# Prompt row tiles found in two waves, with a third strand for the first wave's attention heads

## The reference, cut to what matters

```
def blk(args):                       # 128 query rows at a time, 8 such row tiles
    qb, iqb, iwb, qpos = args
    sc = index_scores(iqb, iwb, ik, key_pos[None, :] <= qpos[:, None])
    vals, idx = lax.top_k(sc, n_sel)             # n_sel = 256
    k_sel, v_sel = k[idx], v[idx]                # abridged
    return sparse_attend(qb, k_sel, v_sel, jnp.isfinite(vals))   # 8 heads

def rwkv7_scan(...):                 # 1024 steps, 4 heads, state S[v, k]
    sa = einsum('bhvk,bhk->bhv', S, at)
    S = S * dt + sa * bt + vt * kt
```

## Time and profile before

| what | value |
|---|---|
| median of 3 runs | 7837.82 us (7829.0 to 7849.85) |
| the profiled execution | 7838.83 us |
| its span, first to last instruction | 7837.1 us |
| busy in the span: TensorE, VectorE, ScalarE | 6192.6, 3201.9, 1222.3 us |
| `stage_prompt_mix`, layer 0 and layer 1 | 963 us each |
| mean granted TensorE clock of the span | 0.799 |

### The profile page before, as it was taken

One profiled execution on the slowest core, in us unless ns is written; L12 is line 12 of the kernel. 1 busy time (PEld: TensorE's weight loads), 2 busy tenths in 40 slices (PEclk: granted clock), 3 DMA queues, 4 the chain that ended last, 5 costly groups with the idle time before them and its releaser, 6 DMA issues. The chain is left out here.

```text
span 7837.1 us, 64844 instructions
## 1 busy us (share of the span) xinstructions
PE 6192.6 (79%) x23434; PEld 3851.3 (49%) x23434; DVE 3201.9 (41%) x7042; ACT 1222.3 (16%) x2304; POOL 737.2 (9%) x776
## 2 busy tenths in 40 slices
PE   7979436558987599999989785365499876999997
PEld 4534324446686445554455334234467863455543
DVE  2246335895452023330032553458944510333300
ACT  2200212112301011110032003121133011111100
POOL 3300000000034400000032000000000353000000
PEclk9989556556667799999999895565567588999999
DMA  4222111000022421112132220110000223211122
GB/s 139 73 75 74 35 31 39 29 13 12 10 59 65 140 106 52 50 53 64 56 112 79 79 70 20 28 48 19 13 18 5 58 76 134 106 56 50 46 73 93
DMA packets 358057, 462.88 MB, mean 59 GB/s; under 512 B 70258, under 2 KB 261172, under 8 KB 357332
## 3 DMA queue, kind: packets, MB, share of 16 engines
q1 hardware_dynamic: 320932, 358.82, 14.2%
q0 software_dynamic: 36864, 100.71, 4.2%
HBM read 347.87 MB, written 121.69 MB: 60 GB/s over the span
## 5 line engine op out<-in xcount | busy, mean ns | idle before, releaser
L395 PE MATMUL pp<-w_in,nT 128*128 128x512 f32 x2016 | 947.0, 618 | 0.0
L2808 PE MATMUL pg<-nT,wgu 128*128 128x512 f32 (+1 forms) x2112 | 709.2, 489 | 17.1 <-DMA wgu<-in_w_up 17.1
L2808 PE MATMUL pu<-nT,wgu 128*128 128x512 f32 (+1 forms) x2112 | 704.4, 487 | 0.0
L2879 PE MATMUL pm<-w_down,hT 128*128 128x512 f32 x1584 | 683.5, 595 | 24.6 <-DMA hT<-scratch_hT 24.6
L2402 POOL DMA_INDIRECT k_sel<-in_cache_k,kv_idx x256 | 243.9, 953 | 4049.8 <-DVE kv_idx L2535 3826.8
L395 PEld LDWEIGHTS pp<-w_in,nT 128*128 128x128 f32 x2016 | 390.8, 199 | 451.4 <-issue 450.7
L2808 PEld LDWEIGHTS pg<-nT,wgu 128*128 128x128 f32 x2112 | 351.6, 192 | 357.3 <-issue 357.3
L2808 PEld LDWEIGHTS pu<-nT,wgu 128*128 128x128 f32 x2112 | 349.8, 191 | 336.6 <-issue 336.6
L2879 PEld LDWEIGHTS pm<-w_down,hT 128*128 128x128 f32 x1584 | 302.2, 191 | 404.6 <-issue 404.6
L2188 DVE TENSOR_SCALAR_CACHE_REDUCE area<-score,cand 128x384 f32<-128x384 f32 x372 | 350.8, 943 | 9.1
L2831 DVE TENSOR_SCALAR sig<-exp_neg 128x512 f32<-128x512 f32 x132 | 47.6, 360 | 722.0 <-ACT exp_neg L2819 722.0
(11 more groups left out here) (581 smaller groups left out, 9128.4 us busy)
## 6 DMA issues: line engine op xcount, KB each, us to landing
w_in<-in_w_in SPq DMA_DIRECT2D x14, 2048.0 KB, 9.3
scratch_hT<-hT SPq DMA_DIRECT2D x44, 576.0 KB, 2.8
hT<-scratch_hT SPq DMA_DIRECT2D x18, 1408.0 KB, 7.4
wgu<-in_w_gate SPq DMA_DIRECT2D x44, 512.0 KB, 3.9
wgu<-in_w_up SPq DMA_DIRECT2D x44, 512.0 KB, 5.2
w_down<-in_w_down SPq DMA_DIRECT2D x22, 1024.0 KB
x_all<-scratch_x SPq DMA_DIRECT2D x27, 512.0 KB, 15.2
a_tile<-scratch_pa SPq DMA_DIRECT2D x18, 516.0 KB, 3.6
```

The costliest lines, as they stand in the source:

```text
L395: ins = pe.matmul(pp[u % 2][:, 0:cw], nT[:, k, t * P:(t + 1) * P], w[:, k, 0:cw], start=(k == 0), stop=(k == KT - 1))
L2808: ins = pe.matmul(bank[:, 0:cw], wb[b][:, which, k, :], nT[:, k, c0:c0 + cw], start=(k == 0), stop=(k == KT - 1))
L2879: ins = pe.matmul(pm[b][n][:, :], h[b][:, k, :], w[:, k, n * 512:(n + 1) * 512], start=(k == 0), stop=(k == FT - 1))
```

## The change

The searched row tiles are put into two waves, tiles 7 and 6, and tiles 5, 4, 3 and 2; the index part takes them in this order. The search is done for the first wave, 32 rounds and its picks, and then for the second. `dsa_strand` becomes `dsa_strands` and gives two strands, select (index, count, pick) and heads. Heads take the row tiles in the order 7, 6, 5, 4, 3, 2, 1, 0. Buffers of the two strands no longer share a tensor: `eq`, `rank`, `s`, `pr`, `pT` are tensors of their own, and the heads' VectorE part has a chain semaphore of its own. The order has three phases:

1. RWKV row tiles 0 and 1 beside the index part of all tiles and the first wave's search;
2. RWKV row tiles 2, 3, 4 beside the second wave's search and the first 32 steps of the heads (16 pairs, the heads of tiles 7 and 6);
3. RWKV row tiles 5, 6, 7 beside the other heads.

```
-def dsa_strand(nc, st, l, io, sc, const, bk):
+def dsa_strands(nc, st, l, io, sc, const, bk):
-    TOPPED = list(range(FIRST, NT))
+    WAVES = ((7, 6), (5, 4, 3, 2))
+    TOPPED = [i for wave in WAVES for i in wave]
+    ORDER = TOPPED + list(range(FIRST - 1, -1, -1))
+    place = {i: n for n, i in enumerate(ORDER)}
...
-    HEADS = [(i, h) for i in range(NT) for h in range(BH)]
+    HEADS = [(i, h) for i in ORDER for h in range(BH)]
...
-    area = st.sb("area", [P, 2, ALL])
-    eq, rank = area[:, 0, :], area[:, 1, :]
-    s = [area[:, 0, b * SEQ:(b + 1) * SEQ] for b in range(2)]
-    pr = [area[:, 0, (2 + b) * SEQ:(3 + b) * SEQ] for b in range(2)]
-    pT = [area[:, 1, b * SEQ:(b + 1) * SEQ] for b in range(2)]
+    eq, rank = st.sb("equal", [P, SEQ]), st.sb("rank", [P, SEQ])
+    s = [st.sb(f"s{b}", [P, SEQ]) for b in range(2)]
+    pr = [st.sb(f"p{b}", [P, SEQ]) for b in range(2)]
+    pT = [st.sb(f"pT{b}", [P, SEQ]) for b in range(2)]
...
-        def settle(r):
+        def settle(r, n0, n1):
+            m = slice(n0, n1)
...
-        for r in range(BITS + 1):
-            for n in range(NTOP):
-                if n == 0 and r:
-                    settle(r - 1)
-                    chain(dve.tensor_tensor(cand[:, :], thr[:, :], bit[:, r - 1:r].to_broadcast([P, NTOP]), ALU.bitwise_xor))
-                count(r, n)
-                yield
-        settle(BITS)
-        for n in range(NTOP):
-            for k in range(3):
-                pick(n, k)
-                yield
+        for wave in WAVES:
+            n0, n1 = TOPPED.index(wave[0]), TOPPED.index(wave[-1]) + 1
+            for r in range(BITS + 1):
+                for n in range(n0, n1):
+                    if n == n0 and r:
+                        settle(r - 1, n0, n1)
+                        chain(dve.tensor_tensor(cand[:, n0:n1], thr[:, n0:n1], bit[:, r - 1:r].to_broadcast([P, n1 - n0]), ALU.bitwise_xor))
+                    count(r, n)
+                    yield
+            settle(BITS, n0, n1)
+            for n in range(n0, n1):
+                for k in range(3):
+                    pick(n, k)
+                    yield
...
+    def heads_vector(dve):
+        chain = Chain(dve, heads_chain_s)
...
-        order = interleave(r_costs, d_costs)
+        tile = (len(r_costs) - 1) // NT
+        r_early, r_late = 2 * tile, 5 * tile
+        order = (interleave(r_costs[:r_early], s_costs[:s_mid], [])
+                 + interleave(r_costs[r_early:r_late], s_costs[s_mid:], h_costs[:h_mid])
+                 + interleave(r_costs[r_late:], [], h_costs[h_mid:]))
```

More of the change, by code:

```diff
@@ L1968, in rwkv_strand @@
     return tile * NT + [2.0], sync, scalar, tensor, vector
-def dsa_strand(nc, st, l, io, sc, const, bk):
+def dsa_strands(nc, st, l, io, sc, const, bk):
     FIRST = TOPK // P
-    TOPPED = list(range(FIRST, NT))
+    WAVES = ((7, 6), (5, 4, 3, 2))
+    TOPPED = [i for wave in WAVES for i in wave]
     NTOP = len(TOPPED)
+    ORDER = TOPPED + list(range(FIRST - 1, -1, -1))
+    place = {i: n for n, i in enumerate(ORDER)}
     BITS = 31
     width = lambda i: (i + 1) * P
-    off = {i: sum(width(j) for j in TOPPED if j < i) for i in TOPPED}
+    off = {i: sum(width(j) for j in TOPPED[:TOPPED.index(i)]) for i in TOPPED}
     ALL = sum(width(i) for i in TOPPED)
@@ L2017, in dsa_strand @@
     po, pt = bk[3], bk[2]
-    loaded, k_loaded, idx_p, idx_r, idx_used, s_p, s_r, mx_r, p_r, pt_p, pt_r, o_p, o_r, chain_s = (st.sem(n) for n in (
-        "ds_loaded", "k_loaded", "idx_psum", "idx_relu", "idx_added", "s_psum", "s_ready", "max_ready", "p_ready", "pT_psum", "pT_ready", "o_psum", "o_ready", "ds_dve_chain"))
+    loaded, k_loaded, idx_p, idx_r, idx_used, s_p, s_r, mx_r, p_r, pt_p, pt_r, o_p, o_r, chain_s, heads_chain_s = (st.sem(n) for n in (
+        "ds_loaded", "k_loaded", "idx_psum", "idx_relu", "idx_added", "s_psum", "s_ready", "max_ready", "p_ready", "pT_psum", "pT_ready", "o_psum", "o_ready", "ds_dve_chain", "heads_dve_chain"))
     stored = [st.sem(f"ds_stored{b}") for b in range(2)]
@@ L2034, in sync @@
         yield
-        for n in range(1, len(costs)):
+        for n in range(1, len(select_costs)):
             if n == 8:
@@ L2041, in sync, with heads_sync @@
                 sp.dma_start(v[:, :, :], sc["v"][0:SEQ, :].rearrange("(t p) n -> p t n", p=P)).then_inc(k_loaded, 16)
+            yield
+    def heads_sync(sp):
+        for n in range(len(heads_costs)):
             if n in out_at:
-                i = out_at[n]
-                sp.wait_ge(o_r, i + 1)
-                sp.dma_start(sc["y"][i * P:(i + 1) * P, AW:AW + BW], o[i % 2][:, :, :].rearrange("p h d -> p (h d)")).then_inc(stored[i % 2], 16)
+                p = out_at[n]
+                i = ORDER[p]
+                sp.wait_ge(o_r, p + 1)
+                sp.dma_start(sc["y"][i * P:(i + 1) * P, AW:AW + BW], o[p % 2][:, :, :].rearrange("p h d -> p (h d)")).then_inc(stored[p % 2], 16)
             yield
@@ L2058, in index, with heads_tensor @@
                 pe.matmul(bk[g % 4][:, 0:cw], iqT[e, h // 2, i * P:(i + 1) * P], ikT[e, c0:c0 + cw], start=True, stop=True).then_inc(idx_p, 1)
+        pe.wait_ge(loaded, 80)
+        for n in range(len(IDX)):
+            index(n)
+            yield
+        yield
+        yield
+        for n in range((BITS + 1) * NTOP + 3 * NTOP):
+            yield
+    def heads_tensor(pe):
         def score(H):
@@ L2083, in values @@
             pe.wait_ge(pt_r, part0[H + 1])
-            if h == 0 and i:
-                pe.wait_ge(o_r, i)
+            if h == 0 and place[i]:
+                pe.wait_ge(o_r, place[i])
             for k in range(i + 1):
@@ L2122, in relu, with heads_scalar @@
                 act.activation(rl[n % 2][:, c0:c0 + cw], bk[g % 4][:, 0:cw], ACT.Relu, scale=HD ** -0.5).then_inc(idx_r, 1)
+        yield
+        for n in range(len(IDX)):
+            relu(n)
+            yield
+        yield
+        for n in range((BITS + 1) * NTOP + 3 * NTOP):
+            yield
+    def heads_scalar(act):
         def expo(H):
@@ L2138, in turned @@
             act.activation(pT[H % 2][:, c0:c0 + cw], pt[:, 0:cw], ACT.Copy).then_inc(pt_r, 1)
[L2140 to L2146, removed]
         for H in range(len(HEADS) + LAG):
@@ L2175, in weigh @@
                 chain(dve.tensor_tensor(last, last, masks[:, CAUSAL_QK, :], ALU.add))
-        def settle(r):
+        def settle(r, n0, n1):
+            m = slice(n0, n1)
             if r == 0:
-                chain(dve.tensor_scalar(thr[:, :], cnt[:, :], TOPK - 0.5, -1.0, ALU.is_lt, ALU.mult))
+                chain(dve.tensor_scalar(thr[:, m], cnt[:, m], TOPK - 0.5, -1.0, ALU.is_lt, ALU.mult))
             else:
-                chain(dve.scalar_tensor_tensor(out=keep[:, :], in0=cnt[:, :], scalar=TOPK - 0.5, in1=bit_f[:, r - 1:r].to_broadcast([P, NTOP]), op0=ALU.is_ge, op1=ALU.mult))
-                chain(dve.tensor_tensor(thr[:, :], thr[:, :], keep[:, :], ALU.bitwise_xor))
+                chain(dve.scalar_tensor_tensor(out=keep[:, m], in0=cnt[:, m], scalar=TOPK - 0.5, in1=bit_f[:, r - 1:r].to_broadcast([P, n1 - n0]), op0=ALU.is_ge, op1=ALU.mult))
+                chain(dve.tensor_tensor(thr[:, m], thr[:, m], keep[:, m], ALU.bitwise_xor))
         def count(r, n):
@@ L2191, in pick @@
             i = TOPPED[n]
-            a, e, r = part(acc, i), part(eq, i), part(rank, i)
+            a, e, r = part(acc, i), eq[:, 0:width(i)], rank[:, 0:width(i)]
             t = thr[:, n:n + 1].bitcast(F32)
@@ L2203, in pick @@
                 chain(dve.tensor_scalar(a, a, -1.0, -NEG, ALU.add, ALU.mult))
+        dve.memset(one[:, :], 1.0)
+        dve.memset(zero[:, :], 0.0)
+        dve.memset(early[:, 0:P], 0.0)
+        chain(dve.tensor_copy(early[:, P:2 * P], masks[:, CAUSAL_QK, :]))
+        dve.wait_ge(loaded, 80)
+        chain(dve.tensor_scalar(iw[:, 1, :, :], iw[:, 0, :, :], IH ** -0.5, None, ALU.mult))
+        yield
+        yield
+        for n in range(len(IDX)):
+            weigh(n)
+            yield
+        for wave in WAVES:
[6 more added lines that the diff above has]
+                    count(r, n)
+                    yield
+            settle(BITS, n0, n1)
+            for n in range(n0, n1):
+                for k in range(3):
+                    pick(n, k)
+                    yield
+    def heads_vector(dve):
+        chain = Chain(dve, heads_chain_s)
+        part = lambda t, i: t[:, off[i]:off[i] + width(i)]
         def mask_and_max(H):
@@ L2208, in mask_and_max @@
                 dve.wait_ge(p_r, H - 1)
-            m_ = mx[i % 2]
+            m_ = mx[place[i] % 2]
             bias = part(acc, i) if i >= FIRST else early[:, 2 * P - width(i):2 * P]
@@ L2221, in finish @@
         def finish(i):
[L2222 to L2238, removed]
-        for r in range(BITS + 1):
-            for n in range(NTOP):
-                if n == 0 and r:
-                    settle(r - 1)
```

(33 more changed lines are left out.)

26 lines of the change are left out of this document (10 added, 16 removed).

## The result

The changed kernel takes 7876.37 us (median of 6 runs, 7859.01 to 7883.75), the kernel before 7838.91 (6 runs): ratio 1.0044, 95% interval 1.0032 to 1.0056. It is slower by 37.5 us. The profiled span is 7874.3 us against 7837.1.

A forecast was written before the change was run, and what follows sets the result against it. The prediction took VectorE to bound the kernel beside counts (89% busy) and TensorE beside heads (93%). A layer summed to 16 + 267 + 345 + 335 + 9 = 972 us against 963, +18 for both: 7857 us, range 7765 to 7935.

The forecast's parts named there:

- Small operations of the second wave: Three VectorE operations ending each count round, 64 times instead of 32, 0.60 us each: +19 us a layer on the path.
- Phase 1: RWKV tiles 0 and 1 beside index and first wave: 267 us (248 to 279), where these tiles took 230.
- Phase 2: RWKV tiles 2 to 4 beside second wave and first heads: 115 us a tile (106 to 130), 345 in all.
- 13 + 9: VectorE's idle time in a phase 2 tile: 13 us as in a count tile, plus 9 for head work.
- the ring: Phase 2: head steps queue ahead of RWKV's products on TensorE, and VectorE waits: 0 to 24 us a tile, 9 taken.
- Phase 3: RWKV tiles 5 to 7 beside 48 heads with 168 key blocks: 335 us, with 315 to 346 considered.
- The free a of the fit: Time of an RWKV tile in the fit for heads, left open by two rows; 61, 85 or 100 us, 85 taken.
- Sum: A layer at 16 + 267 + 345 + 335 + 9 = 972 us against 963: +9, +18 for both layers.
- The signs: Expected in the trace: tile 2 starting at 1546, tiles 2 to 4 at 110 to 120 us, VectorE busy 90 to 95.
- Overlap works: Rival: heads fit TensorE's idle half and its clock rises; 919 us a layer, 7751 us full, 7795 half way; chance 0.29.
- TensorE bound at its lower clock: Rival: TensorE stays slow and becomes the bound, phase 2 at 130 us a tile; 7981 us full size; chance 0.19.
- half way: Half-size case of a rival; for TensorE as the bound at its lower clock it was put at 7920 us.

The follow-up runs named there:

- two-wave run: Changed kernel with its two waves kept but no third strand, heads following select in one strand as in the kernel before: 0.9984 of the kernel before.
- half-size steps: Changed kernel with each head's scores and products by v cut into two steps: 0.9976 of the kernel before; with scores later too, 0.9826.
- the same exchange: Kernel before with two TensorE calls exchanged, products by v in a pair's first step and scores in the second: 0.9861 of the kernel before.
- scores later: Scores asked for one step later, products by v one step earlier, on TensorE: changed kernel 0.9866, two waves without third strand 0.9883 of the kernel before.

## Why the prediction was right, and which term was too small

The direction and the range were right; the size was +18 us and is +37.5. The two layers grew by 48 us together; that the whole grew by less lies outside the stage and is within the spread of the runs.

- *Small operations of the second wave.* I put +19 us of VectorE a layer on the path. VectorE is busier by 15 us in the whole stage, L2194 (L2182 before) appears 62 times a layer as against 31 and still takes 161 ns, so the price holds within 4 us. That it lies on the path does not: the two-wave run absorbed 12 us in idle time.
- *Phase 1.* 258 and 262 us against 267 (248 to 279). VectorE is busy 225 of them, where the terms add up to about 230 (69 in the index part and 161), and idles 33 to 36 us where they left 37.
- *Phase 2.* This is the mis-sized term. VectorE's 93 us a tile are 90; its idle time, "13 + 9", is 29 to 34 in layer 0. A tile took 122 and 125 us on average, not 115, inside 106 to 130. The working named the ring (head work queued ahead of RWKV's products) but priced it by the length of the head's work, from tiles where no counts stood in VectorE's queue, and went to the lower end because counts would fill VectorE's wait. The runs showed another link, by which the counts work the other way: the scores' wait for VectorE, 38 us in 13 pieces, which the counts in VectorE's queue make long. Taking it away shortened phase 2 by 30 us at nearly the same clock, and by 41 in layer 1, where the clock rose too. The length of the head's work is a link too: 26 us less of it shortened phase 2 by 7 and 13. The wait was in the trace before as the longest of the heads on TensorE, 16.9 us in 17 pieces of at most 2.1. The prediction gave that entry no row and no price. A change that puts counts ahead of L2214 could be expected to lengthen it.
- *Phase 3.* 339 and 328 against 335. The free a of the fit is measured now, 75 us, and with it the fit gives 327 us. So 335, which lies between the two layers, came from a choice of a that no row had shown, and that it fits so well is luck: tile 5 alone took 130 us in one layer and 112 in the other.
- *Sum.* Layer 0: −9 (phase 1), +22 (phase 2) and +4 (phase 3) on the predicted +9 give the measured +26. Layer 1: −5, +29 and −7 give +26 too; measured are +22, since its tiles took 942 us before and the sum starts from layer 0's 938. The span has 11 us less elsewhere.
- *The signs.* VectorE's 90 to 91 us a tile came true; tile 2 started at 1534, not 1546, and tiles 2 to 4 took 119 to 128 us, most of them over the 110 to 120 that I had named. In the rivals' prices, half way from 7839 to 7981 is 7910, not 7920.
- *The rivals.* Overlap works: not as the code stood. The Trainium skill's rule ("Perfetto Trace Analysis", Optimization Strategy: interleaving regimes with different most-contended engines may pay) was not refuted: with the wait gone the change is 0.9866 and, with half-size steps, 0.9826. But the kernel before with the same exchange is at 0.9861, so interleaving the regimes alone brought nothing that can be told apart. TensorE bound at its lower clock: the clock was 0.60 to 0.63 in phase 2, between the two cases, but TensorE was busy only 250 to 261 of 368 to 375 us, so it was not full. Its lower clock cost something all the same: layer 1's phase 2 has the same instructions as layer 0's, TensorE busy 12 us longer at 0.60 and 7 us more time.

Whether the third strand pays by itself stays open. With scores later it is 9 us a layer ahead of the two-wave kernel without it by the medians (7996 and 8015 us) and 7 by the layers, but level with the kernel before (0.9866 and 0.9861), and the intervals overlap in both pairs. Only the kernel with half-size steps (0.9826) is clear of the kernel before with the same exchange, and half-size steps were tried only with the third strand.

## What to carry to other kernels

When strands share in-order engines, list the waits that cross engines within one step before adding a strand: a wait on a result of the same step pins the engine that would run ahead to the slower one's place in the order, and every strand behind it pays. Ask for a buffer one step after the step that frees it. Price such a wait by what will stand ahead of its releaser, not by its size in the old trace.

## What the runs showed that was not expected

Heads alone kept TensorE busy 331 of 337 us at a granted clock of 0.50 (1.2 GHz); index work alone ran at 1.00 while busy 45 of 48 us. The same heads beside RWKV's products ran at 0.72. And an exchange of two calls that removed 17 us of waits from a layer took 48 us off it, nearly all of it TensorE's busy time: the clock of one tile went from 0.67 to 0.83 with it.
